# A hybrid encoder step whose last expert stage works densely on 384 token columns instead of 416

## The reference

```python
def _peer(h, w_pq, sub_keys, u_experts, v_experts):      # per block of tokens xb
    s = einsum('thcd,hckd->thck', query(xb), sub_keys)   # 8 heads, 2 halves, 128 keys
    sv, si = top_k(s, 16)
    cand = sv[:, :, 0, :, None] + sv[:, :, 1, None, :]
    top_s, top_pos = top_k(cand, 16)
    eid = 128 * row_key + col_key                        # 16384 experts
    gate = softmax(top_s)
    act = gelu(einsum('thkd,td->thk', u_experts[eid], xb))
    return einsum('thk,thkd->td', gate * act, v_experts[eid])
```

## Time and profile before

| | |
|---|---|
| median of 3 runs | 4732.21 us (4726.02 to 4737.42) |
| the profiled execution, its own time | 4726.86 us |
| its span, first to last instruction | 4725.1 us |
| TensorE busy | 4618.4 us, 98% |
| VectorE busy | 2667.7 us, 56% |
| GpSimd busy | 1393.9 us, 30% |
| ScalarE busy | 1240.8 us, 26% |
| granted TensorE clock, mean | 0.991 |

### The profile page before, as it was taken

The page is one execution under the profiler, slowest core; times in us unless marked ns, Lnnn a source line. Parts: engine busy times, 40 slices in busy tenths (PEclk is TensorE's granted clock), DMA queues, the critical chain, the costliest instruction groups (busy, mean ns, idle before and its releaser), DMA issues.

```text
span 4725.1 us, 81398 instructions
## 1 busy us (share of the span) xinstructions
PE 4618.4 (98%) x32961; PEld 4531.9 (96%) x32961; DVE 2667.7 (56%) x3838; ACT 1240.8 (26%) x1275; POOL 1393.9 (30%) x668
## 2 busy tenths in 40 slices
PE   8999999989999999999999999999999999999998
PEld 8999988879996999999999999999999999999998
DVE  4445566552322233656677777710008998989985
ACT  4233343322312231222221111212222222222223
POOL 0000001011000100233343333333345565656633
PEclk9999999989999999999999999999999999999999
DMA  3243432335664566654456556665458777777763
GB/s 143 83 159 117 149 125 100 105 133 175 177 216 130 176 180 196 204 166 152 150 162 193 172 181 190 185 199 193 151 168 308 293 298 283 297 297 303 285 232 135
DMA packets 513009, 893.10 MB, mean 189 GB/s; under 512 B 30080, under 2 KB 409344, under 8 KB 443264
## 3 DMA queue, kind: packets, MB, share of 16 engines
q1 hardware_dynamic: 220032, 623.03, 37.7%
q10 hardware_dynamic: 270336, 134.25, 10.5%
q0 software_dynamic: 22528, 134.30, 7.2%
HBM read 790.88 MB, written 234.82 MB: 217 GB/s over the span
## 4 chain that ended last, share of the span: by engine, by line
PE 57%; issue 9%; POOL 1%; DVE 0%; ACT 0%; POOLq 0%; ACTq 0%; DVEq 0%
PE pu L250 44%; PE pm L250 12%; PE pm L1346 1%; POOL sumsq L1701 1%; POOL sumsq L307 0%; PE pm L1252 0%; POOL wlo L239 0%; DVE y_out L1666 0%; DVE clo L1571 0%; ACT squares L1637 0%; PE pu L1721 0%; PE pm L1259 0%; ACT L1643 0%; PE pm L1555 0%; PE pu L1555 0%
## 5 line engine op out<-in xcount | busy, mean ns | idle before, releaser
L250 PE MATMUL pu<-xhi,whi 128*128 128x272 f32 x7456 | 1548.6, 289 | 30.0 <-DVE xlo L480 12.3
L250 PE MATMUL pu<-xhi,wlo 128*128 128x272 f32 x7456 | 1545.6, 289 | 0.0
L250 PE MATMUL pu<-xlo,whi 128*128 128x272 f32 x7456 | 1540.5, 288 | 0.0
L250 PEld LDWEIGHTS pu<-xhi,whi 128*128 128x128 f32 x7456 | 1174.7, 189 | 33.8 <-issue 24.1
L250 PEld LDWEIGHTS pu<-xlo,whi 128*128 128x128 f32 x7456 | 1174.9, 189 | 0.0
L250 PEld LDWEIGHTS pu<-xhi,wlo 128*128 128x128 f32 x7456 | 1167.2, 189 | 0.0
L234 ACT CAST whi<-raw 128x2048 fp32r<-128x2048 f32 x397 | 757.2, 1907 | 1496.0 <-PE pm L250 838.3
L239 POOL TENSOR_TENSOR wlo<-raw,whi 128x2048 fp32r<-128x2048 f32 x128 | 611.7, 4779 | 1192.0 <-ACT whi L234 1192.0
L239 DVE TENSOR_TENSOR wlo<-raw,whi 128x2048 fp32r<-128x2048 f32 x269 | 627.9, 2334 | 414.7 <-ACT whi L234 408.0
L250 PE MATMUL pu<-chi,whi 128*128 128x416 f32 (+1 forms) x1056 | 366.1, 347 | 3.8 <-DVE clo L1571 3.0
L250 PE MATMUL pm<-chi,wlo 128*128 128x416 f32 (+1 forms) x1056 | 368.7, 349 | 0.0
(11 more groups left out here) (316 smaller groups left out, 4934.7 us busy)
## 6 DMA issues: line engine op xcount, KB each, us to landing
raw<-units SPq DMA_DIRECT2D x397, 1024.0 KB, 5.1
v_rows<-units ACTq DMA_DIRECT2D x512, 256.0 KB, 6.6
h_s<-h_out SPq DMA_DIRECT2D x128, 272.0 KB, 3.4
gate_s<-table SPq DMA_DIRECT2D x13, 2048.0 KB, 9.5
h_in<-h_s SPq DMA_DIRECT2D x32, 832.0 KB, 6.4
gate_in<-gate_s SPq DMA_DIRECT2D x32, 832.0 KB, 8.8
x<-xT SPq DMA_DIRECT2D x8, 1088.0 KB, 6.3
q_s<-q_out SPq DMA_DIRECT2D x32, 272.0 KB, 4.7
```

The costliest lines, as they stand in the source:

```text
L250: ins = nc.tensor.matmul(out, w, xs[b][m == 1], start=(first and n == 0 and m == 0), stop=(last and n == len(terms) - 1 and m == 2))
```

## The change

- `ND`, the number of dense columns in the output stage, goes from 416 to 384. The table has 12 chunks instead of 13, with as many hidden units in all.
- The fourth chunk of the routing (tokens 384 to 511) is kept as lists as well, but only its first 32 tokens are used. Four small transfers pack them: partition 32 s + r holds token 384 + r and slots 32 s to 32 s + 31. So 32 more gathers of 128 values and 32 more gathers of 128 rows serve those 32 tokens.
- The first 128 slots are spread over groups 0 to 22 (five or six in each), the 32 packed ones over groups 23 to 28. `row_sum` is turned and added to `x` in pair 12 (`FIRST_OUT`), used again for the packed slots, and in the last pair TensorE sums its four quarters with a selection matrix (32 columns) and VectorE adds them in one instruction.
- In each pair but the last the units of two groups alternate, and their 8 key blocks are summed in one PSUM tile: VectorE adds 16 tiles in a pair instead of 32.
- `pool_gate` writes its product over `coef_in`, so it no longer waits for `clo_ready`. `chi` and `clo` get a third buffer. `load_group` waits for `clo_ready`. Gates, roundings and remainders of the first two groups are made ahead of the first pair.
- The rounding of the even group stands at the pair's second unit, that of the odd group at its eighth.
- In the last units the first sum of squares (`total(0)`) is taken one unit later, and the first part of the output starts one unit later. The parts are 416 and 128 columns wide instead of 384 and 160.

```diff
-GT = 128
-ND = T - GT
+GT = P
+G1 = T - GT
+ND = G1 - TS
...
-        routed(NCH - 2, ND, GT)
+        routed(NCH - 2, G1)
...
+            if m == STRETCH - 1:
+                sp.wait_ge(slots_kept, 1)
+                for s in range(PACK):
+                    sp.dma_start(packed[TS * s:TS * (s + 1), 0:3], kept[0:TS, :, PACKED * s:PACKED * (s + 1)]).then_inc(slots_packed, 16)
...
-            nc.gpsimd.tensor_tensor(coef[:, q], h_in[s][:, q], gate_in[s][:, :, q], ALU.mult).then_inc(coef_ready, 1)
+            nc.gpsimd.tensor_tensor(coef_in[s][:, q], coef_in[s][:, q], gate_in[s][:, :, q], ALU.mult).then_inc(coef_ready, 1)
...
-        pool_gate(pool, 0, 0, 1)
+        for s in (0, 1):
+            pool_gate(pool, s, s, 1)
...
-    ROW_GROUPS = 28
+    SET_GROUPS = [range(0, 23), range(23, 29)]
+    SET_SIZE = [SLOTS, PACKED]
...
+            if e:
+                ins = nc.tensor.matmul(SUM_OUT[0][:, k * TS:(k + 1) * TS], row_sum[:, k], consts[:, C_SEL:C_SEL + TS], start=True, stop=True)
...
+    def unit_pe(pe, i, r, n, tile, side, cols, opens=True, closes=True, fresh=False, within={}):
...
+            products([out_slot(side, d)[:, cols]],
+                     [(whi[:, slot, GRP * d + k], wlo[:, slot, GRP * d + k], [(chi[b][:, k, cols], clo[b][:, k, cols])]) for k in range(GRP)],
+                     first=opens, last=closes, before=operand_ready if fresh and d == 0 else None).then_inc(tiles_done, 1)
...
+                unit_pe(pe, i, 2 * j + r, n, 4 * (n // 2), side_of(n, False), slice(0, ND), opens=r == 0, closes=r == 1, fresh=n < 2,
+                        within={2: lambda: pe_sums(pe, 0, i)} if first_out and n == 0 else {})
...
+                if last:
+                    add_tile(dve, i, n, 4 * w + d, side_of(n, True), PART[0] if n >= VU else slice(0, ND))
+                elif n % 2:
+                    add_tile(dve, i, n, 4 * (n // 2) + d, side_of(n, False), slice(0, ND))
...
     def experts_sync(sp):
         hidden_stage_sync(sp)
-        pairs(sp, pair_sp)
+        for s in (0, 1):
+            sp.wait_ge(h_stored[s], 8 * P + PRIME)
+        sp.wait_ge(clo_ready, GRP)
+        load_group(sp, 2, 0)
+        for i in range(END + 1):
+            pair_sp(sp, i, i == END)
...
-            unit_pe(pe, END, 1, 2 * VU + w, PART[1], within={3: lambda: total(0)} if w == 0 else {})
+            unit_pe(pe, END, 1, n, 4 * n, side_of(n, True), PART[1], within={3: lambda: total(0)} if w == 1 else {})
```

More of the change, by code:

```diff
@@ L79 @@
 C_VALID = C_CNT + 64
[L80 to L81 removed]
+C_SEL = C_VALID + NCH * HEADS
+C_TOK = C_SEL + TS
+NC = C_TOK + 2
 def constants():
@@ L1453, in stretch @@
                 hidden_pe(pe, 0, STRETCH, t, m, before=lambda n: between(m, n))
-        with pe.Fori(0, NCH - 1) as t:
+        with pe.Fori(0, NCH - 2) as t:
             stretch(t, True)
-        stretch(NCH - 1, False)
+        with pe.Fori(NCH - 2, NCH) as t:
+            stretch(t, False)
         with pe.Fori(0, TCH) as c:
@@ L1491, in hidden_stage_vector @@
             assert chain.n == ROUTE_LINKS, chain.n
[L1492 to L1495, removed]
+        chain.enter(NCH - 2, ROUTE_LINKS)
+        for which in (1, 0):
+            dve_route(dve, NCH - 1 - which, chain, kept_as=which)
+        dve.wait_ge(slots_kept, 2)
+        dve.wait_ge(slots_taken, NCH + PRIME)
         dve.wait_ge(x_parked, 16 + X_LOADED)
@@ L1573, in act_coef, with dve_sums @@
[L1573 to L1592 removed]
+    def dve_sums(dve, e):
+        dve.wait_ge(sample_out, e + 1)
+        if e:
+            nc.vector.tensor_tensor(x[:, :, ND:G1], SUM_OUT[0][:, 0:KT * TS].rearrange("p (k n) -> p k n", k=KT), x[:, :, ND:G1], ALU.add)
+            return
+        for n, bank in enumerate(SUM_OUT):
+            at = slice(4 * n, 4 * n + 4)
+            nc.vector.tensor_tensor(x[:, at, G1:T], bank[:, 0:4 * GT].rearrange("p (k n) -> p k n", k=4), x[:, at, G1:T], ALU.add)
@@ new lines, in build @@
+    source_of = lambda m: VU * (m % 2) + m // 2
+    def pair_sp(sp, i, last):
+        for m in range(2 * VU):
+            if m < 2 * VU - 2:
+                source = None if last else i * (2 * VU) + (V0 + source_of(m + 2))
+            elif last:
+                source = UNITS - 3 * VU + m + 2
+            else:
+                source = i * (2 * VU) + (V0 + 2 * VU + (source_of(m + 2 - 2 * VU) if i < END - 1 else m + 2 - 2 * VU))
+            load_unit(sp, i * (2 * VU) + (V0 + m + 2), (V0 + m) % 2, source)
+            if m == 0 and not last:
+                sp.wait_ge(clo_ready, i * (2 * GRP) + 2 * GRP)
+                load_group(sp, i * 2 + 3, 1)
+            if m == VU and i < END - 1:
+                sp.wait_ge(clo_ready, i * (2 * GRP) + 3 * GRP)
+                load_group(sp, i * 2 + 4, 0)
@@ L1703, in pairs @@
     def pairs(eng, pair):
-        with eng.Fori(0, NGRP // 2 - 1) as i:
-            pair(eng, i, False)
-        pair(eng, NGRP // 2 - 1, True)
+        with eng.Fori(0, END // CYCLE - 1) as i:
+            for j in range(CYCLE):
+                pair(eng, i * CYCLE + j, j, False)
+        for i in range(END - CYCLE, END):
+            pair(eng, i, i % CYCLE, False)
+        pair(eng, END, 0, True)
     def experts_sync(sp):
         hidden_stage_sync(sp)
-        pairs(sp, pair_sp)
+        for s in (0, 1):
[4 more added lines that the diff above has]
+            pair_sp(sp, i, i == END)
         for b in (0, 1):
@@ L1776, in experts_gpsimd @@
         pool.wait_ge(rows_laid, 16 * GRP * P + X_LOADED)
-        for i in range(NGRP // 2):
-            pair_pool(pool, i, i == NGRP // 2 - 1)
+        for i in range(END + 1):
+            pair_pool(pool, i, i % CYCLE, i == END)
     residual_and_projection(1, MO0, V_FFN, experts=dict(
```

268 lines of the change are left out of this document (147 added, 121 removed).

## The result

| | before | after |
|---|---|---|
| median of 5 runs each | 4733.9 us (4726.02 to 4737.42) | 4706.95 us (4702.19 to 4713.19) |
| ratio, with its 95% interval | | 0.9942 (0.9931 to 0.9954) |
| span of the profiled execution | 4725.1 us | 4705.1 us |

The change makes the kernel faster by 27 us, 0.6%. The forecast was 4646 us, 86.7 us less than before, with a range of 4629 to 4676. The sign is right; the time is off by 61 us, and lies 31 us outside the range.

The account below looks back on a forecast made before the run. TensorE was taken to set the pace, with VectorE and the transfers close behind. Terms summing to -86.7 us took the profiled 4726.9 to 4640.2; the runs' median lies 5.4 higher, giving 4646 us, range 4629 to 4676.

Parts of the forecast that it names:

- the term for the waits: Output stage: small waits from late rows and VectorE held by GpSimd's gates, +3 us, between 0 and +12.
- 5.06 without: GpSimd's four gates: 9.21 us beside VectorE work with two SBUF inputs, 5.06 us without such work.
- The transfers: Output stage: rival that transfers set the pace, 347 GB/s needed; at a limit of 330, 4685 us; 6 in 100.
- The GpSimd loop: Output stage: rival that GpSimd sets the pace, late rows holding VectorE, then TensorE; 4658 to 4681 us; 16 in 100.
- slower than before: Output stage: rival that late rows open TensorE gaps, half clock following; all 15 pairs +134 us, 4780; 4 in 100.
- The columns: Output stage: 5952 full-width products each 14.6 ns shorter, saving 86.9 us, bounds 79.4 and 95.8.
- The start: Start of the output stage: first gates, roundings and remainders delay unit 1's cast, +2.5 us, between 0 and +4.
- The end: Last units: first sum of squares a unit later removes TensorE's 6.51 us wait; -3 us, between -7 and +2.
- The sums: Pair 12: new turn of `row_sum`, 16 products, +1.75 us, between +0.9 and +3.5.
- Wait for nothing that is late: Pair 12: VectorE's additions wait for nothing late, since TensorE's third unit needs them a unit later.
- The table: Table products: twelve chunks instead of 13, 4 units become plain, saving 3.7 us.

Follow-up runs that it names:

- the last experiment: Changed kernel with row gathers of 512 of 2048 values, gate products of 32 of 384 columns, and TensorE's loops written out: 4639.14 us.
- the rows and gates together: Changed kernel with row gathers of 512 of 2048 values from the sixth on and gate products of 32 of 384 columns: 4658.69 us.
- the fastest version: Changed kernel with gate products moved to VectorE, a group's load in four parts and TensorE's loops written out: 4645.87 us.
- short gates: Changed kernel with each output-stage gate product doing 32 of its 384 columns: 4664.34 us.
- short rows: Changed kernel with row gathers fetching 512 of 2048 values from the sixth on: 4679.1 us.

## Why the prediction was wrong, point by point

The prediction named the test that it fails: casts as far apart as forecast (8.32 us, 8.37 forecast) and a total off by more than 15 us.

**The step that failed** is the term for the waits: "I take +3 for small waits, between 0 and +12". The runs put 68 us there, the main part of the changed kernel against that of the last experiment (1110.5 and 1042.5): VectorE held by GpSimd's gates, `raw` landing late, and the loop's turn, with half clock behind many of the gaps that TensorE has from them. By its parts, as they come off one by one: the rows and gates together 49, then the loop's turns 19. Three things were in the prediction and were not joined.

- *A held VectorE.* The prediction quoted the contention, and priced it on GpSimd's side alone (four gates in 5.06 or 9.21 us). VectorE's side stood in the earlier trace rows: a tiny product of 3.74 us, ended with the gates. So "5.06 without" misreads the rows: that product has two SBUF inputs, and those gates were quick because it was the one held. The hold was priced as a small delay, not as 4.7 us in a slack of 4.1.
- *The transfers*, a rival at 6 in 100 and 4685 us, "fits, barely". The rate does fit: up to 412 GB/s in a slice, 349 from 3600 to 4200 us in the fastest version (and the highest slice in the earlier trace rows is 371, not 367). What moved is the landing of `raw`, 4.9 to 8.0 us at the median, and 1.57 MB in front of it in the queue. The rival was right that `raw` would be waited for, and wrong to price it by the mean rate. The Trainium skill's figure of about 358 GB/s for one core ("DMA: Bandwidth & Descriptors", section "Where 436 GB/s comes from") is not borne out by these slices.
- *The GpSimd loop*, at 16 in 100: it named the wait (TensorE for `wlo`), not the reason. Its sign, `row_sum` waiting for `rows`, did not come (1.1 us in 127 rows). Its price counted 14 groups with six rows among the 23; there are 13.

**The loop's turn** was in no part of the prediction, though the change says that TensorE's loop holds three pairs instead of one. 10.8 us of gaps, and 19 us in the main part when the rest is out of the way.

**The half clock** was named, in the rival "slower than before", with 8.95 us for a gap of 6.5. It comes after gaps of 2.2 to 4.6 us too, and costs 19 us in all. TensorE's gaps from 3545 to 4560 us were 32, and 17 of them under 1 us; the rival's sum of 134 us was far too high.

**The columns**: 86.9 forecast, 92.7 measured, inside the bounds and nearer to the upper one. The Trainium skill's rule ("TensorE: Matmul & The Clock Gate", section "Wait — 56ns, not 53.3ns?") gave the lower bound of 79.4; the row at 384 columns is 173.3 ns, 13.3 over 160.0, so its constant of about 2.5 doesn't hold here.

**The start**: +2.5 forecast. From the last `h_out` to the end of unit 0 it was 12.6 us with a unit of 9.07, and is 15.7 with one of 8.32: +3.9, inside the bounds, but not by the wait forecast. TensorE waits for `clo` four times in unit 0 and then runs in part at half clock (a granted clock of 0.73 from 3537 to 3545 us):

```profile
3532.03 0.44 PE L254 MATMUL pu<-chi,whi 128*128 128x384 f32 x1 [1.96 <-DVE clo L1614]
3533.50 0.44 PE L254 MATMUL pu<-chi,whi 128*128 128x384 f32 x1 [0.68 <-DVE clo L1614]
3534.96 0.69 PE L254 MATMUL pu<-chi,whi 128*128 128x384 f32 x1 [0.68 <-DVE clo L1614]
```

**The end**: -3 forecast, -3.8 measured (68.3 to 64.5). The gap of 6.51 us of the earlier trace rows is gone; instead there are small ones of 1.2 to 1.4 us before the last units, and

```profile
4694.67 0.49 PE L1796 MATMUL pu<-sumsq,consts 128*128 128x128 f32 x2 [2.01 <-POOL sumsq L1768]
```

**The sums**: +1.75 forecast for the turn. There is also a gap of 3.06 us in pair 12: TensorE's third unit waits for an addition that VectorE reaches only behind the four additions of `row_sum` and the first rows of the new set. "Wait for nothing that is late" was wrong for this one.

**The table**: -3.7 forecast, -3.1 measured, though the hidden stage ended 2.9 us later. Its first `h_out` already came 5.7 us later (1931.09 and 1936.83), and from its 40th, the last before the table's units, to its last it is 1106.9 us before and 1103.8 after: -3.1. A turn of TensorE's loop ahead of that adds two gaps, 3.0 us. Why the stage starts later stays open.

**The rest of the sum** holds up. With 92.7 for the columns the same terms give 4640 us, and with nothing held 4639.14 was measured. That the two agree to 1 us is luck: with short gates unit 0 ends 12.2 us after the last `h_out`, so most of the start's +3.9 isn't in that run, and the hidden stage's end alone moves by 14 us between profiles. The forecast was one for a kernel whose VectorE isn't held, whose loads don't queue and whose loop doesn't stop.

Open is how the 30 us that come only with both divide. Short gates also take load off GpSimd, so that it asks for rows sooner, and short rows take load off the transfer engines for every queue.

## What to carry to other kernels

When the bounding engine gets faster, compare the slack of each hand-over in one period (here 4.1 us) with the longest single hold that can fall on it, a neighbour's run of instructions or the transfer ahead in the queue, not with mean busy shares: two delays that cost little alone meet. Work that holds its neighbour can be cheaper on the busier engine: 95 us of products moved to VectorE gained 51. When a written-out loop body grows, look for waits a fixed period apart, under whatever name the profile gives them, and look at the weight loads' rows too.

## What the runs showed of the hardware that was not expected

- VectorE can be blocked for the whole of four GpSimd instructions in a row, even with an instruction of 5 columns: 4.65 us for what takes 0.15 to 0.16 alone. Not always: in four of thirty such runs the four gates take 12.2 to 12.4 us instead, with VectorE's work in turns between them. What decides it stays open.
- A turn of TensorE's loop with 1152 products in it leaves a gap of 2.7 to 4.6 us; the loop with 384 products left none.
- The granted clock falls to 0.50 behind gaps of 2.2 to 4.6 us (eight of the ten over 2 us in the changed kernel's main part), not only after the 6.51 us of the earlier trace rows; it stays at 1.00 behind two others there, of 2.11 and 2.22 us, and behind one of 3.07 us in the last experiment.
- The transfer engines moved 405 to 420 GB/s over stretches of 5 to 7 us.
- A gate product, with a stride of four values on one input, takes VectorE 856 ns at 384 columns where a remainder of the same width takes 552 to 556.
